# DeltaNet: projected blocks between the steps of one staggered run of 24 chunk units

## The reference, cut to what matters

```
def project(h):                                   # h: (tokens, 1024)
    p = h @ w_in                                  # q, k, v, z: 8 heads x 128 each; a, b
    qkv = silu(centred_dwconv(p[..., :3072], conv_w))          # 5 taps
    q, k = l2norm(q) * 128**-0.5, l2norm(k)
    g, beta = -exp(a_log) * softplus(a + dt_bias), sigmoid(b)
...
def step(s, inp):                                 # over the chunks, for each head and direction
    v_new = u_n - w_n @ s
    o_n = qd_n @ s + qk_n @ v_new
    s = s * exp(gl_n) + kd_n.T @ v_new
...
o = rmsnorm(o_forward + o_backward, norm_g) * silu(z)
y = o @ w_out
```

## Time and profile before

| | us |
|---|---|
| median of 3 runs | 4268.17 (4264.69 to 4269.55) |
| span of the profiled execution | 4263.6 |
| TensorE, VectorE, ScalarE, GpSimd busy in it | 3903.4, 2098.1, 1607.7, 562.6 |
| matmuls of lines 233 to 235, projections from weights (first group of the page) | 1047.0 + 1028.0 + 1027.1 |
| small fp32 matmuls, line 230 | 802.7 |

### The profile page before, as it was taken

One profiled execution on the slowest core, in us unless ns is written; L12 is line 12 of the kernel. 1 busy time (PEld: TensorE's weight loads), 2 busy tenths in 40 slices (PEclk: granted clock), 3 DMA queues, 4 the chain that ended last, 5 costly groups with the idle time before them and its releaser, 6 DMA issues.

```text
span 4263.6 us, 67437 instructions
## 1 busy us (share of the span) xinstructions
PE 3903.4 (92%) x28266; PEld 3208.1 (75%) x28266; DVE 2098.1 (49%) x3022; ACT 1607.7 (38%) x2639; POOL 562.6 (13%) x628
## 2 busy tenths in 40 slices
PE   6988897878999998988899989999999998899999
PEld 4866686766888776756688766677888887678887
DVE  3545454656221353267523664454655427655564
ACT  3333333333111233155322335644334336554333
POOL 0035303642000001002100000000220003000220
PEclk8988898888999999999899999999999999999999
DMA  5234433131221122101233230131223330322232
GB/s 155 82 130 144 149 97 115 35 100 50 70 70 60 55 71 69 60 11 57 94 98 99 79 85 21 42 129 51 91 97 99 95 108 15 112 79 77 93 103 85
DMA packets 248534, 355.08 MB, mean 83 GB/s; under 512 B 9299, under 2 KB 158502, under 8 KB 247846
## 3 DMA queue, kind: packets, MB, share of 16 engines
q1 hardware_dynamic: 233840, 300.49, 21.9%
q0 software_dynamic: 13840, 50.11, 3.7%
q10 hardware_dynamic: 550, 0.17, 0.0%
HBM read 336.50 MB, written 14.24 MB: 82 GB/s over the span
## 4 chain that ended last, share of the span: by engine, by line
PE 77%; DVE 12%; ACT 7%; issue 2%; POOL 2%; DMA 1%; ACTq 0%; DVEq 0%; SPq 0%; POOLq 0%
PE psum L233 20%; PE psum L234 20%; PE psum L235 20%; PE psum L230 14%; ACT arena L341 3%; DVE arena L264 3%; PE psum L239 3%; DVE arena L274 2%; DVE rw L264 2%; DVE rx L335 2%; ACT arena L345 1%; POOL arena L379 1%; DVE arena L278 1%; ACT rw L345 1%; DVE arena L270 1%
## 5 line engine op out<-in xcount | busy, mean ns | idle before, releaser
L233 PE MATMUL psum<-rx,rw 128*128 128x512 f32 (+2 forms) x2864 | 1047.0, 366 | 54.9 <-DVE rx L335 28.8
L234 PE MATMUL psum<-rx,rw 128*128 128x512 f32 (+2 forms) x2864 | 1028.0, 359 | 0.0
L235 PE MATMUL psum<-rx,rw 128*128 128x512 f32 (+2 forms) x2864 | 1027.1, 359 | 0.0
L264 DVE TENSOR_TENSOR rw<-arena,rw 128x2048 fp32r<-128x2048 f32 (+2 forms) x239 | 537.5, 2249 | 828.8 <-ACT rw L345 822.9
L230 PE MATMUL psum<-arena 32*32 32x32 f32 (+10 forms) x12982 | 802.7, 256 | 148.0 <-ACT arena L345 63.8
L230 PEld LDWEIGHTS psum<-arena 32*32 32x32 f32 (+5 forms) x12982 | 608.7, 140 | 322.5 <-ACT arena L345 102.2
L345 ACT ACTIVATE rw<-arena 128x2048 fp32r<-128x2048 f32 (+2 forms) x239 | 448.1, 1875 | 753.9 <-PE psum L235 730.0
L233 PE MATMUL psum<-rw,rx 128*128 128x512 f32 (+1 forms) x1720 | 681.2, 396 | 45.2 <-DVE rx L335 27.2
L234 PE MATMUL psum<-rw,rx 128*128 128x512 f32 (+1 forms) x1720 | 671.5, 390 | 0.0
L235 PE MATMUL psum<-rw,rx 128*128 128x512 f32 (+1 forms) x1720 | 671.5, 390 | 0.0
L233 PEld LDWEIGHTS psum<-rx,rw 128*128 128x128 f32 (+1 forms) x2864 | 549.2, 192 | 156.4 <-DVE rx L335 42.4
(11 more groups left out here) (71 smaller groups left out, 2091.3 us busy)
## 6 DMA issues: line engine op xcount, KB each, us to landing
arena<-in_ffn_w_up SPq DMA_DIRECT2D x66, 1024.0 KB, 5.1
arena<-in_ada_w SPq DMA_DIRECT2D x48, 1024.0 KB, 5.2
arena<-in_ffn_w_down SPq DMA_DIRECT2D x40, 1024.0 KB, 5.0
arena<-in_ffn_w_gate SPq DMA_DIRECT2D x22, 1024.0 KB, 5.1
arena<-in_dn_w_in SPq DMA_DIRECT2D x32, 512.0 KB, 5.4
arena<-in_xa_w_kv SPq DMA_DIRECT2D x16, 1024.0 KB, 5.1
arena<-in_hgrn_w_in SPq DMA_DIRECT2D x16, 1024.0 KB, 5.5
arena<-in_da_w_in SPq DMA_DIRECT2D x12, 1024.0 KB, 5.2
```

What stands on the lines that cost most here:

```text
L233: self.e.matmul(out, l[0], r[0], start=start, stop=False)
L234: self.e.matmul(out, l[0], r[1], start=False, stop=False)
L235: return self.e.matmul(out, l[1], r[0], start=False, stop=stop)
L264: return self.e.tensor_tensor(out, a, b, op)
```

## The change

The order of the blocks is new (`STREAM`): K and Q of two heads by turns, then V, for the first group, the same for the second, and the 8 Z blocks last. A weight tile holds two neighbouring heads of one kind (256 columns). The first 12 blocks are computed as before, one behind another (`DENSE`). All 24 units then form one run of 138 rounds, without meets. Between the rounds of units, `*_between` does the other 20 blocks in pieces by the number of the round, one block per 5 rounds until round 100: TensorE 4, 2, 2 + 4 and 4 k-steps in four of five rounds, VectorE two and three taps, ScalarE and VectorE quarters of the weight split. `ada` steps stand at rounds 0 and 2 of each 5, then at every second round to 117. `ada` tiles have one raw slot, the blocks' tiles the other. Units, `ada` and posts share PSUM banks 0 to 5, the pieces of blocks use 6 and 7.

k by token and v by token are no longer kept in SBUF: every k and v block is stored, and each unit loads its k (as it did v) two rounds before use; for that a unit has one more round. k and q of the second group by feature are stored too (`kq_s`), and loaded chunk by chunk over those of the first group from round 50 on. The tails run per token chunk instead of per head (12 of them, rounds 101 on, the last within `dn_out`), write their halves directly where `dn_out` reads them, and `o_s` is gone. `dn_out` takes the token tiles of its first half in the order in which they are ready. The constants and rows for the layer norm behind it are loaded at its start, as before.

```diff
@@ TensorLane
-    def bank(self, *key):
-        while self.ptr % 8 in self.held:
-            self.ptr += 1
-        i = self.ptr % 8
-        self.ptr += 1
+    def bank(self, *key, among=tuple(range(8))):
+        j, n = self.ptr.get(among, 0), len(among)
+        assert not self.held.issuperset(among)
+        while among[j % n] in self.held:
+            j += 1
+        i = among[j % n]
+        self.ptr[among] = j + 1
...
@@ VectorLane (ScalarLane: the same, for the high half)
+    def split_quarter(self, t, q):
+        raw, (hi, lo) = self.K.tile_raw(t), self.K.wview(t, 2048, 1)
+        self.wait_ge(*self.K.at("hi", t, q))
+        part = slice(q * 512, q * 512 + 512)
+        self.tt(lo[:, 0, part], raw[:, part], hi[:, 0, part].bitcast(F32), SUB).then_inc(*self.sig(("lo", t)))
...
@@ the order of the blocks
-PARTS = [(h4, part) for h4 in range(4) for part in (K_, Q_, V_, Z_)]
+KQ = [(h + i, part) for h in (0, 2) for part in (K_, Q_) for i in range(2)]
+STREAM = ([(0,) + x for x in KQ] + [(0, h, V_) for h in range(4)] + [(1,) + x for x in KQ] + [(1, h, V_) for h in range(4)]
+          + [(hg, h, Z_) for hg in range(2) for h in range(4)])
+DENSE = 12
+LAST_Q = (7, 19)
+UNIT_BANKS, PART_BANKS = (0, 1, 2, 3, 4, 5), (6, 7)
...
@@ one block, or a piece of it
+def pe_part_steps(p, K, r, m, s, ks, among):
+    o, size = DN_SEGS[s]
+    key, w = ("dn", r, s), K.wview(m, 256, 8)
+    b = p.bank(*key, among=among) if ks[0] == 0 else K.ps(*key)
+    f = block(r % 2, 128)
+    for k in ks:
+        ins = p.mm3(b[:, 0:size], [x[:, k, f] for x in w], K.toks(k, o, size), k == 0, k == 7)
+    if ks[-1] == 7:
+        ins.then_inc(*p.sig(key, ("used", m)))
+        p.close(*key)
...
@@ the rounds
-def staggered(units, side, each=None):
-    units, live, rnd = list(units), [], 0
-    while units or live:
+def before_unit(hg, n):
+    return EVERY_UNIT[12 * hg + n - 2] if 12 * hg + n >= 2 else None
+def rounds(units, between):
+    live, units = [], list(units)
+    for rnd in range(ROUNDS):
         if units and rnd % GAP == 0:
             live.append(units.pop(0))
         for u in list(live):
             if next(u, "end") == "end":
                 live.remove(u)
-        rnd += 1
-        if rnd % 2 == 0:
-            next(side, None)
-        if each:
-            each(rnd)
+        between(rnd)
...
+def part_rounds(rnd, offset):
+    r = DENSE + (rnd - offset) // GAP
+    return r if (rnd - offset) % GAP == 0 and DENSE <= r < len(STREAM) else None
+STEPS = {0: ((0, (0, 1)), (0, (2, 3))), 1: ((0, (4, 5)),), 2: ((0, (6, 7)), (1, (0, 1, 2, 3))), 3: ((1, (4, 5, 6, 7)),)}
+TILE_ROUNDS = range(0, 90, 10)
+SIDE_ROUNDS = [r for r in range(100) if r % 5 in (0, 2)] + list(range(101, 119, 2))
+KQ_ROUNDS = {50: 4, 51: 5, 61: 2, 66: 1, 71: 3, 76: 0}
+TAILS = ((101, 0, 5), (104, 0, 4), (107, 1, 5), (110, 0, 2), (113, 1, 4), (116, 0, 1), (119, 0, 3), (122, 0, 0), (125, 1, 2),
+         (129, 1, 1), (134, 1, 3), (139, 1, 0))
+TAIL_ORDER = (5, 4, 2, 1, 3, 0)
...
@@ what each engine does between two rounds (ScalarE and GpSimd likewise)
+def pe_between(p, K, side, ms, rnd):
+    for i, hg, c in tail_rounds(rnd, 3):
+        pe_tail(p, K, i, hg, c, PART_BANKS)
+    if rnd < 2:
+        pe_part_post(p, K, DENSE - 2 + rnd, UNIT_BANKS)
+    r = part_rounds(rnd, 9)
+    if r is not None:
+        pe_part_post(p, K, r, UNIT_BANKS)
+    if rnd == 48:
+        pe_G_rows(p, K, 1, UNIT_BANKS)
+    if rnd in SIDE_ROUNDS:
+        next(side, None)
+    if rnd in TILE_ROUNDS:
+        ms.append(p.take((0, part_weights(K, DENSE + 2 * len(ms))), slot=0, pieces=True))
+    r = DENSE + rnd // GAP
+    if r < len(STREAM):
+        m = ms[(r - DENSE) // 2]
+        p.wait_ge(*K.at("lo", m))
+        for s, ks in STEPS.get(rnd % GAP, ()):
+            pe_part_steps(p, K, r, m, s, ks, PART_BANKS[s:s + 1])
...
+    r = part_rounds(rnd, 5)
+    if r is not None and STREAM[r][2] != Z_:
+        dve_conv(v, K, r, (0, 1))
+    r = part_rounds(rnd, 7)
+    if r is not None and STREAM[r][2] != Z_:
+        dve_conv(v, K, r, (2, 3, 4))
...
@@ pool_unit, pe_unit
+    heads_stored(g, K, hg, K_)
+    g.load(("k",) + U, [(r2(B[4], 4), K.k_s[c, :, hg * 4:hg * 4 + 4, :])], f"k{n % 4}")
+    yield
     yield
+    g.wait_ge(*K.at("k", *U))
-    g.tt(r2(B[4], 4), khat[:, :, c, :], bcl(of_unit(kd, d, c, hg), 128), MUL).then_inc(*g.sig(("kd",) + U))
+    g.tt(r2(B[4], 4), r2(B[4], 4), bcl(of_unit(kd, d, c, hg), 128), MUL).then_inc(*g.sig(("kd",) + U))
...
@@ dn_out
+def pe_dn_out(p, K):
+    W, hs, bs, ms = K.I["dn_w_out"][0], out_chunks(8), {}, {}
+    for c, (h, k0, kn) in enumerate(hs):
+        ms[c] = p.tile((0, W[k0 * 128:(k0 + kn) * 128, h * 512:(h + 1) * 512]))
+        w = K.wview(ms[c], 512, kn)
+        order = range(6) if h else TAIL_ORDER
+        for t in order:
+            if h == 0:
+                p.wait_ge(*K.at("o_lo", c, t))
+            if (c, t) == (0, TAIL_ORDER[4]):
+                pe_tail(p, K, LAST, *TAILS[LAST][1:], EVERY)
+            if k0 == 0:
+                bs[t, h] = p.bank("dn_out", t, h)
+            for k in range(kn):
+                ins = p.mm3(bs[t, h][:, :], K.toks(k0 + k, t * 128, 128), [x[:, k, :] for x in w], k0 + k == 0, k0 + k == 7)
+            if k0 + kn == 8:
+                ins.then_inc(*p.sig(("dn_out", t, h), ("used", ms[c])))
+                p.close("dn_out", t, h)
+            elif t == order[-1]:
+                ins.then_inc(*p.sig(("used", ms[c])))
...
@@ pe_program (the other programs likewise)
-    side = (step for i, pc in SIDE for step in pe_ada(p, K, i, pc))
+    side = (step for i, pc in SIDE for step in pe_ada(p, K, i, pc, UNIT_BANKS, 1))
     pe_gates(p, K, t1)
-    for hg in range(2):
-        pe_dn_proj(p, K, hg)
-        p.meet(f"dn_proj{hg}")
-        staggered([pe_unit(p, K, hg, n) for n in range(12)], side)
-        if hg:
-            for step in side:
-                pass
-        p.meet(f"delta{hg}")
-    pe_out(p, K, "dn_out", K.I["dn_w_out"][0], 8, 6, ("o_lo",), turn=pe_tail_turn(p, K))
+    pe_dn_proj(p, K)
+    ms = [p.take((0, part_weights(K, DENSE)))]
+    rounds([pe_unit(p, K, hg, n) for hg, n in EVERY_UNIT], lambda rnd: pe_between(p, K, side, ms, rnd))
+    for step in side:
+        pass
+    pe_dn_out(p, K)
     yield "ln1"
     pe_turn(p, K, t2, 0, "ln1_row")
     pe_swiglu(p, K, "g0", 0, 6, t2, "ln1_row")
```

More of the change, by code:

```diff
@@ L148, in wview, with tile_added, tile_raw, tile_before @@
     def wview(self, m, n, k, off=0):
-        i = m % 2
+        i = self.rws[m] % 2
         return [self.rw[:, i * 4096 + j * RS + off:i * 4096 + j * RS + off + k * n].rearrange(
             "p (k n) -> p k n", n=n) for j in range(2)]
+    def tile_added(self, pts, slot=None, raw=False, pieces=False):
+        m = len(self.tiles)
+        self.tiles.append(pts)
+        self.slots.append(slot if slot is not None else 1 - self.slots[-1] if m else 0)
+        self.rws.append(m - len(self.raw))
+        if raw:
+            self.raw.add(m)
+        if pieces:
+            self.pieces.add(m)
+    def tile_raw(self, m):
+        return self.mem(self.slots[m] * RS, tile_words(self.tiles[m]))
+    def tile_before(self, m):
+        old = [t for t in range(m) if t not in self.raw and self.rws[t] == self.rws[m] - 2]
+        return old[0] if old else None
     def at(self, *key):
@@ L245, in tile, with raw_tile @@
         if self.K.rehearsing:
-            self.K.tiles.append(pts)
+            self.K.tile_added(pts, **kind)
+        return m
+    def tile(self, *pts):
+        m = self.take(*pts)
         self.wait_ge(*self.K.at("lo", m))
         return m
[L250 to L256, removed]
+    def raw_tile(self, *pts, slot=None):
+        m = self.take(*pts, slot=slot, raw=True)
         self.wait_ge(*self.K.at("landed", m))
@@ L395, in weights @@
                                  allow_slow_non_contiguous=True).then_inc(sem, 16)
-            K.book["landed", t] = (sem, 16 * sum(len(x) for x in K.tiles[i:t + 1:2]))
+            K.book["landed", t] = (sem, 16 * sum(len(K.tiles[u]) for u in here))
 def tile_words(pts):
@@ L845, in dve_out @@
 def dve_out(v, K, tag, Kn, nt, src=None, gate=None, between=(), after=None, made=0, have=None, begun=0,
-            old=None, late=False):
+            old=None, late=False, first=None):
     between, end = dict(between), len(out_chunks(Kn))
@@ L858, in dve_out @@
         if k0 + kn == Kn:
-            for t in range(nt):
+            for t in first if first and h == 0 else range(nt):
                 xs, ps = K.X[:, t, h * 512:(h + 1) * 512], K.ps(tag, t, h)[:, :]
@@ L4233, in dve_program @@
     for part in range(2):
[L4234 removed]
+        pipeline([dve_ada(v, K, 0, pc, v.tile) for pc in ADA_FIRST[2 * part:2 * part + 2]], 2, 1)
         for g in range(2):
             dve_turn(v, K, t1, g, part)
[L4237 removed]
+    side = (step for i, pc in SIDE for step in dve_ada(v, K, i, pc, v.skip))
     v.tile()
```

901 lines of the change are left out of this document (529 added, 372 removed).

## The result

The changed kernel takes 4192.95 us (median of 4, 4191.21 to 4204.73) against 4268.86 us of the kernel before on the same chip (4264.69 to 4278.35): a ratio of 0.9825, 95% interval 0.981 to 0.9839. It is faster by 76 us, where 135 were forecast. The profiled execution took 4192.13 us, its span is 4190.3 us. The experiments further down ran on several chips; on these the kernel before took between 4268.38 and 4271.55 us, and each ratio is against the kernel before on the same chip. The four times of the changed kernel lie 13.5 us apart, so a smaller difference of a single run shows little. First the page's head, which answers to the earlier trace rows.

The account below looks back on a forecast made before the run. TensorE, busy for 92%, was taken to bound the kernel. Terms 99 + 490 + 111 + 66 = 766 us against 901, 135 less, gave 4133 us; range 4085 to 4225.

Parts of the forecast that it names:

- What bounds the kernel: Whole kernel: TensorE busy for 92% of 4263.6 us, so only its work, idle time or clock can give time.
- (a): Dense part before the run of units: 12 blocks at 8.25 us each, 99 us.
- (d): `dn_out` at the end: 65 us as before plus 1; the 17 us between the stages go.
- (b): Rounds 0 to 99, units with 20 blocks and `ada`: 442 us of work at yield 0.90, so 490 us.
- a stretch like 776 to 780: Unit rounds before: some 4 us with TensorE nearly idle, then clock 0.50; blocks as filler should prevent it.
- (c): Rounds 100 to 137, last four units, remaining `ada` and tails: 111 us, bounds 104 and 122.
- Bank ring: PSUM banks, 6 for units and 2 for blocks: TensorE's waits for evictions cost 0, at most 1 us per gap.
- Rival 1: Rounds 0 to 99 without idle time at clock 1.00: 442 us instead of 490, total 4085; chance 0.10.
- Rival 2: Rounds 0 to 99 keep present idle share and low clock: 593 us, total 4236, half of it 4184; chance 0.16.
- Rival 3: Rounds 0 to 99: all 40 ScalarE table loads on the path, +51 us, total 4184; chance 0.06.
- Rival 4: Rounds 0 to 99: each round's non-TensorE chain adds to all TensorE work, 661 us, total 4304; chance 0.07.
- no effect: Unit run: units wait for blocks until the order is serial again, total 4250 to 4268; chance 0.03.

Follow-up runs that it names:

- two taps: Changed kernel with only 2 of 5 convolution taps in the 12 streamed K, Q and V blocks (values then wrong): 4158.74 us, one run.
- all three: Changed kernel with eight tails earlier, Z blocks read out a round earlier, and weight-split low halves on GpSimd instead of VectorE: 4148.9 us, ratio 0.9714.

## Why the prediction was right in kind and off in size

- **What bounds the kernel**: right. The time went from TensorE's idle time and clock: busy time in this part fell by 15 us only (778.8 to 763.7), the stretch by 72.
- **(a) Dense part**: 100 against 99, by luck. "16 blocks took 132 us" holds for 14 blocks. 12 blocks at 8.25 and the 10 blocks at 10.0 that the window really holds give nearly the same.
- **(d) `dn_out`**: right, 67 against 66. The twelfth tail is hidden, TensorE is busy for all 67 us. Its last unit matmuls end 3.6 us ahead of `dn_out`, where 2 were forecast; between the two stand the transposes of the eleventh tail.
- **(b), the work**: the term that was mis-sized most in (b). "20 blocks x 8.25 = 165" became 192 (9.6 each), while units and `ada` took 268 instead of 277: 460 us at full clock instead of 442. At the forecast's own idle time and clock that alone makes 510 us where 490 were forecast, 20 of the 28 us missed.
- **(b), the yield**, the share of the time that is work at full clock: nearly right in size, 460/518 = 0.89 for "5% idle and a clock of 0.95, a yield of 0.90". The other 8 us come from it. But its size was assumed, and the step beside it failed: "None exceeds 27.4, so I cost them at nothing; what hides them is TensorE's 24.7". Most of the loss of 58 us is VectorE's pieces: leaving out 36 taps brings it to 23, moving the splits to 27. That the assumed 48 came near was luck. A busy share below one did not hide them here, since each engine runs its list in order: a piece delays the unit steps behind it in that round (the 2.14 us at 386 above). The 27.4 and 24.7 are also per unit of work done (divided by 17.9), not per gap of 5 rounds: 490/20 is 24.5, and there was less room than the comparison has. The loss per gap in us, with the length of rounds 0 to 99 and the work at full clock (busy time by clock) in the first rows:

| | before the pieces (all blocks first) | changed | splits on GpSimd | all three | two taps | forecast |
|---|---|---|---|---|---|---|
| rounds 0 to 99, us | 362 | 518 | 488 | 482 | 482 | 490 |
| work at full clock, us | 268 | 460 | 462 | 461 | 459 | 442 |
| loss per gap, us | 4.7 | 2.9 | 1.3 | 1.0 | 1.2 | 2.4 |

  My mark for "wrong", VectorE above 75% in rounds 5 to 65, was not reached (74% there; 145.3 of 194, 74.9%, in rounds 25 to 59). It was set too high, since the harm was there at that share.
- **"So that a stretch like 776 to 780 should not recur"**: wrong, 388 to 400 is one, though TensorE had blocks. They stood in that round behind the unit steps that VectorE was late with.
- **(c), the end of the run**: the largest mis-sized term, 144 for 111. "I put 7 on the path": tails alone cost 28, since each is a chain through four engines beside those of the last units. TensorE's 7 us of transposes, from which I sized them, is the wrong measure. The other 12 lie in the units and `ada`; how they split was not tested.
- **Bank ring**: "0, at most 1 us per gap" stays open: one bank less costs 13 us over 20 gaps, 0.65 each.
- **Rival 1, full cover**: didn't come. Its 442 was short of the work; two taps and no table loads together take 475 us for 459 of work.
- **Rival 2, half of the loss**: the nearest in time, 4184 against 4193, and its mechanism (convolution pieces in order between unit steps) is shown. That the total is so near is partly luck, since 33 us of the miss lie in the end of the run, which it leaves alone. It had 0.16, and deserved more: the prediction named it and then costed those pieces at nothing.
- **Rival 3, table loads**: out, 4.6 us instead of 51 in one run (8 by the ratios). By the rule of the Trainium skill ("ScalarE: Activation LUTs", section "What ACT_TABLE_LOAD costs") they would have been 106 us on the path; no run here shows its drain, and with or without one the 40 loads cost less than 10 us.
- **Rival 4, lock-step**, and no effect: out.

Where the 76 us come from: one run in the place of two stages, with all blocks ahead of it, brings 0.72%, 31 us; putting the blocks between the rounds brings the other 1.03%, 44. Two costs of the former are not of its kind: its blocks take 200 us where 20 at 9.4 would take 189, and it waits up to 24 us for the weights of `ada`. Without them it could bring up to 66 us and the pieces as little as 10 (an estimate, not run). So the single run has between 31 and 66 of the 76 us, and the forecast never priced it apart from the pieces.

## What to carry to other kernels

Before you put independent work between the steps of a latency-bound chain, count its pieces on every in-order engine of the chain, and charge two thirds or more of their time (here 34 of 50 us and 26 of 29), even where that engine is busy for less than its share of the gap; move those pieces first that can go to an engine which has slack and whose result is needed late. Size a tail of small steps by its chain, not by the busy time of the engine that bounds the rest. Count the blocks in a window by their records before you divide by them. And compare with the plain version that only removes the barriers: here it had 31 of the 76 us as it stood, and perhaps more.

## What the runs showed of the hardware

VectorE and GpSimd slow each other down on f32 work from SBUF, both at once. In the timeline of the changed kernel (start, length, instruction), first one tap with GpSimd idle, then three beside three GpSimd products of 128x512:

```profile
309.24 1.02 DVE L299 SCALAR_TENSOR_TENSOR arena<-arena 128x770 f32<-128x770 f32 x1
...
316.68 4.93 POOL L454 TENSOR_TENSOR arena<-arena 128x512 f32<-128x512 f32 x3 [2.12 <-DVE arena L295]
317.72 4.71 DVE L299 SCALAR_TENSOR_TENSOR arena<-arena 128x770 f32<-128x770 f32 x3
```

The tap takes 1.02 us alone and 4.71/3 = 1.57 beside GpSimd; a product takes at most 4.93/3 = 1.64 beside the taps. In the two-tap kernel, where those taps are left out, the same three products take 3.58 us, 1.19 each:

```profile
317.76 3.58 POOL L454 TENSOR_TENSOR arena<-arena 128x512 f32<-128x512 f32 x3 [2.12 <-DVE arena L295]
```

And work taken from TensorE does not all come back as time: of 49.6 us of matmuls left out of rounds 60 to 99 31 turned into idle time and a lower clock, 0.85 instead of 0.95, in one run.
